# A three-term sum of w_down's weights made and stored during the up product, and a convolution tap moved from GpSimd to ScalarE

## What is computed

```python
def causal_depthwise_conv(u, w, b):
    C = u.shape[-1]
    y = lax.conv_general_dilated(u, w[:, None, :].astype(u.dtype), window_strides=(1,),
                                 padding=[(CONV_WIDTH - 1, 0)],
                                 dimension_numbers=('NWC', 'WIO', 'NWC'),
                                 feature_group_count=C)
    return y + b
...
        h = rms_norm(x, ffn_norm_g)
        u = causal_depthwise_conv(h @ w_up, conv_w, conv_b)
        gate, val = jnp.split(u, 2, axis=-1)
        x = x + (jax.nn.silu(gate) * val) @ w_down
```

## Time and profile before

| | us |
|---|---|
| median of 3 runs (1435.15 to 1435.22) | 1435.2 |
| the profiled execution | 1435.17 |
| its span, first to last instruction | 1433.3 |
| TensorE busy in the span | 1427.8 |
| VectorE busy | 1138.3 |
| ScalarE busy | 841.5 |
| GpSimd busy | 448.0 |

### The profile page before, as it was taken

How to read it: one execution, slowest core, us unless ns; L and a number is a source line. 1 busy time by engine, 2 the same in 40 slices (tenths; PEclk the granted TensorE clock), 3 DMA queues, 4 the chain that set the end, 5 groups by cost and what they waited for, 6 DMA issues and landing times.

```text
span 1433.3 us, 23700 instructions
## 1 busy us (share of the span) xinstructions
PE 1427.8 (100%) x7626; PEld 1222.9 (85%) x7626; DVE 1138.3 (79%) x1503; ACT 841.5 (59%) x1181; POOL 448.0 (31%) x493
## 2 busy tenths in 40 slices
PE   9999999999999999999999999999999999999999
PEld 7888888888888888888888888888888888888887
DVE  6778998886656566899967778777778778999998
ACT  7545667666767666666664455455554545465553
POOL 2310000333132213650025455655556555200000
PEclk9999999999999999999999999999999999999999
DMA  8565665655554545567555565566665565566664
GB/s 260 187 197 172 209 195 186 193 176 176 161 162 160 167 170 178 189 221 234 192 178 184 183 202 181 186 191 190 190 191 185 180 198 185 192 232 206 204 207 148
DMA packets 121063, 272.25 MB, mean 190 GB/s; under 512 B 10688, under 2 KB 10976, under 8 KB 121008
## 3 DMA queue, kind: packets, MB, share of 16 engines
q1 hardware_dynamic: 119936, 268.99, 58.1%
q0 software_dynamic: 896, 2.42, 0.6%
q10 hardware_dynamic: 176, 0.14, 0.0%
HBM read 269.42 MB, written 2.10 MB: 189 GB/s over the span
## 4 chain that ended last, share of the span: by engine, by line
PE 99%; DMA 0%; DVE 0%; DVEq 0%; issue 0%
PE bank L2098 98%; PE bank L2152 1%; DMA y<-in_x 0%; PE bank L2371 0%; PE bank L2412 0%; DVE y L1770 0%; PE bank L2235 0%; PE bank L2171 0%; PE bank L2213 0%; DVE y L1815 0%; DVEq L201 0%; PE bank L2220 0%; PE bank L2210 0%; PE bank L2202 0%; DVEq L529 0%
## 5 line engine op out<-in xcount | busy, mean ns | idle before, releaser
L1100 DVE TENSOR_TENSOR lo<-raw,hi 128x1024 fp32r<-128x1024 f32 (+1 forms) x342 | 444.3, 1304 | 167.0 <-ACT hi L639 166.3
L639 ACT ACTIVATE hi<-raw 128x1024 fp32r<-128x1024 f32 (+1 forms) x342 | 359.2, 1053 | 271.6 <-PE bank L2098 266.9
L2098 PE MATMUL bank<-h2T,hi 128*128 128x512 f32 x1408 | 483.3, 394 | 0.0
L2098 PE MATMUL bank<-h2T,lo 128*128 128x256 f32 x1408 | 376.8, 278 | 0.0
L2098 PEld LDWEIGHTS bank<-h2T,hi 128*128 128x128 f32 x1408 | 257.9, 188 | 53.5
L2098 PE MATMUL bank<-hT,hi 128*128 128x512 f32 (+1 forms) x784 | 272.9, 395 | 0.0
L2098 PEld LDWEIGHTS bank<-h2T,lo 128*128 128x128 f32 x1408 | 264.4, 188 | 7.8
L2098 PE MATMUL bank<-hT,lo 128*128 128x256 f32 (+1 forms) x784 | 212.6, 281 | 0.0
L2062 POOL TENSOR_TENSOR u<-u,rms_row 128x256 f32<-128x256 f32 x88 | 120.9, 1374 | 184.7 <-DVE u L1621 165.7
L2098 PE MATMUL bank<-hi,ffT 128*128 128x512 f32 x576 | 177.4, 389 | 0.0
L2098 PEld LDWEIGHTS bank<-hT,hi 128*128 128x128 f32 (+1 forms) x784 | 143.9, 187 | 29.4
(11 more groups left out here) (292 smaller groups left out, 2017.6 us busy)
## 6 DMA issues: line engine op xcount, KB each, us to landing
raw<-in_w_up SPq DMA_DIRECT2D x176, 512.0 KB, 3.5
raw<-in_w_in SPq DMA_DIRECT2D x160, 512.0 KB, 3.4
raw<-in_w_down SPq DMA_DIRECT2D x88, 512.0 KB, 4.4
raw<-in_w_branch SPq DMA_DIRECT2D x32, 512.0 KB, 3.6
raw<-in_w_out SPq DMA_DIRECT2D x24, 512.0 KB, 4.6
raw4h<-in_w_in SPq DMA_DIRECT2D x8, 512.0 KB, 3.4
raw5h<-in_w_in SPq DMA_DIRECT2D x8, 512.0 KB, 4.4
raw45m<-in_w_out SPq DMA_DIRECT2D x8, 512.0 KB, 4.9
```

The source lines that it names most:

```text
L639: act.activation(hi[s][:, 0:width], raw[s][:, 0:width], ACT.Copy)\
L1100: dve.tensor_tensor(lo[s][:, 0:width], raw[s][:, 0:width], hi[s][:, 0:width].bitcast(f32), ALU.subtract)\
L2098: return pe.matmul(o, l, r, start=start, stop=stop, skip_group_check=True)
```

## The change

Two things are changed. First, the weight sums of the pairs 8 to 15, for both halves m, are made during up: in each of the groups n = 1 to 8, SP loads the rows of one pair for each half into `pre0` and `pre1` (three DMAs, 1 MB each half), VectorE makes three sums in place (`pre_sums`), and SP stores them (1 MB each half) to a tensor `sums` in HBM. In down the 16 merged steps of these pairs (`stored`) load four chunks (256 KB and 3 x 512 KB) in place of two, and make no sums. Pairs 14 and 15 are merged as well, in both halves, by a sixth batch: 8 merged pairs in the first half, 12 in the second. Only the four merged pairs 0 to 3 of the second half still sum on VectorE. The order of steps is new: 5 plain pairs and then merged and plain in turn 8 times, one plain; the batches' due times are moved to match. Second, in up the third tap is no longer GpSimd's but an activation of ScalarE with the tap as scale (`last_tap`), which for a value tile adds the value bias in the same instruction (Identity with a bias); GpSimd keeps the scaling and the product with silu. The diff, cut to its core:

```diff
-               Batch(10, 2, (5, 0), (5, 1), (6, 0), (6, 1), (7, 0)),
-               Batch(12, 2, (9, 0), (10, 2), (12, 2), (13, 0), (14, 2)),
-               Batch(0, 2, (19, 0), (19, 1), (20, 0), (21, 0), (21, 1)),
-               Batch(2, 2, (25, 2), (27, 2), (29, 2), (30, 0), (31, 2))]
+               Batch(10, 2, (4, 1), (5, 2), (6, 0), (6, 1), (7, 2)),
+               Batch(12, 2, (8, 0), (8, 1), (9, 2), (10, 0), (10, 1)),
+               Batch(14, 2, (11, 2), (12, 0), (12, 1), (13, 2), (14, 0)),
+               Batch(0, 2, (15, 2), (16, 0), (16, 1), (17, 2), (18, 0)),
+               Batch(2, 2, (29, 2), (30, 0), (30, 1), (31, 2), (32, 0))]
     SUMMED = [b.pair + j for b in BATCHES for j in range(b.count)]
+    STORED_AT, STORED = 8, 8
...
-        first = [(0, k, None) for k in range(8)]
-        for i in range(6):
-            first += [(0, SUMMED[i], i), (0, 14 + i, None)]
-        first += [(0, k, None) for k in (20, 21)]
-        rest = [k for k in range(PAIRS) if k not in SUMMED]
-        second = [(1, rest[0], None)]
-        for i in range(10):
-            second += [(1, SUMMED[i], i), (1, rest[i + 1], None)]
-        second += [(1, rest[11], None)]
-        table, chunk = [], C_DOWN
-        for i, (m, pair, made) in enumerate(first + second):
-            table.append(Step(m, pair, made, chunk, 2 * i))
+        first = [(0, k, None) for k in range(5)]
+        for i, k in enumerate((5, 6, 7, 16, 17, 18, 19, 20)):
+            first += [(0, SUMMED[i], i), (0, k, None)]
+        first += [(0, 21, None)]
+        second = [(1, k, SUMMED.index(k) if k in SUMMED else None)
+                  for k in (6, 8, 0, 7, 9, 1, 16, 10, 17, 11, 18, 12, 2, 19, 13, 3, 20, 14, 21, 15,
+                            4, 5)]
+        table, chunk, raw = [], C_DOWN, 0
+        for m, pair, made in first + second:
+            stored = made is not None and STORED_AT <= pair < STORED_AT + STORED
+            table.append(Step(m, pair, made, chunk, raw, stored))
             chunk += 2 if made is None else 4
+            raw += 4 if stored else 2
...
+        pre = [at(f"pre{m}", [4 * GRP], (72 + 8 * m) * KB) for m in range(2)]
+        sums = nc.dram_tensor("sums", (2 * STORED * P, 4 * GRP), f32, kind="Internal").ap()
...
+            def pre_load(m, n):
+                wait_alone(sp, pre_stored[m], 16 * n - 15)
+                row, col = 2 * P * n + 2 * P * (STORED_AT - 1), m * BLOCK
+                sp.dma_start(pre[m][:, 0:2 * GRP], w_down[ds(row, P), col:col + BLOCK])\
+                    .then_inc(pre_landed[m], 16)
+                sp.dma_start(pre[m][:, 2 * GRP:3 * GRP],
+                             w_down[ds(row + P, P), col + GRP:col + BLOCK])\
+                    .then_inc(pre_landed[m], 16)
+                sp.dma_start(pre[m][:, 3 * GRP:4 * GRP], w_down[ds(row + P, P), col:col + GRP])\
+                    .then_inc(pre_landed[m], 16)
+            def pre_store(m, n):
+                wait_alone(sp, pre_summed, 6 * n - 3 + 3 * m)
+                sp.dma_start(sums[ds(P * n + (m * STORED - 1) * P, P), :], pre[m][:, :])\
+                    .then_inc(pre_stored[m], 16)
+            prime(sp, *pre_stored)
+            for b in range(2):
+                load_group(C_UP + b * CPG, w_up, 0, b * FF)
+            wait_alone(sp, rms_done, 2)
+            with sp.Fori(1, STORED + 1) as n:
+                for b in range(2):
+                    for j in range(CPG):
+                        if (b, j) in ((0, 0), (0, 4)):
+                            pre_load(j // 4, n)
+                        wait_alone(sp, lo_done, C_UP + b * CPG + j - AHEAD + 2 * CPG * n)
+                        rows = w_up[j * CK * P:(j + 1) * CK * P, ds(b * FF + GRP * n, GRP)]
+                        load(j % SLOTS, raw[j % SLOTS][:, :].rearrange("p (k c) -> p k c", k=CK),
+                             rows.rearrange("(k p) c -> p k c", p=P))
+                        if (b, j) in ((1, 3), (1, 7)):
+                            pre_store(j // 4, n)
+            for m in range(2):
+                wait_alone(sp, pre_stored[m], 16 * STORED + 1)
+            with sp.Fori(STORED + 1, NU) as n:
                 for b in range(2):
                     load_group(C_UP + b * CPG, w_up, 2 * CPG * n, b * FF + GRP * n)
...
+                width = GRP if step.stored and k == 0 else BLOCK
+                if k < 2:
                     kt = 2 * step.pair + k
-                    load(RAW_SLOT[q], raw_down[RAW_SLOT[q]][:, :],
-                         w_down[kt * P:(kt + 1) * P, step.m * BLOCK:(step.m + 1) * BLOCK])
+                    src = w_down[kt * P:(kt + 1) * P, step.m * BLOCK:step.m * BLOCK + width]
+                else:
+                    row = (step.m * STORED + step.pair - STORED_AT) * P
+                    src = sums[row:row + P, (k - 2) * BLOCK:(k - 1) * BLOCK]
+                load(slot, raw_down[slot][:, 0:width], src)
...
+            def last_tap(b, n, ct):
+                e = 4 * n + ct
+                scaled, done = ((gate_scaled, gate_w2), (val_scaled, val_w2))[b]
+                if b == 0 and (not isinstance(e, int) or e >= 2):
+                    act.wait_ge(silu_done, e - 1)
+                if b == 1 and ct >= 2:
+                    act.wait_ge(ffT_done, e - 1)
+                act.wait_ge(scaled, e + 1)
+                tap = params[:, ds(2 * KT + 2 * FT * 2 + b * FT + e, 1)]
+                if b == 0:
+                    act.activation(conv[b][ct % 2][:, :], u[b][ct][:, 2:S + 2], ACT.Copy,
+                                   scale=tap).then_inc(done, 1)
+                else:
+                    act.activation(conv[b][ct % 2][:, :], u[b][ct][:, 2:S + 2], ACT.Identity,
+                                   bias=params[:, ds(2 * KT + 3 * 2 * FT + FT + e, 1)],
+                                   scale=tap).then_inc(done, 1)
             def up_step(n, j):
 
                 if j < 4:
                     val_half(n - 1, j)
+                if j in (1, 3, 5, 7):
+                    last_tap(1, n - 1, j // 2)
...
+                if j in (1, 3, 5, 7):
+                    last_tap(0, n, j // 2)
...
+                if step.stored:
+                    down_hi(step.chunk + 2, weights_in(step.raw + 2))
+                    between(i, 2)
+                    down_hi(step.chunk + 3, weights_in(step.raw + 3))
+                    return
...
+                    if storing and j in (1, 2, 3, 5, 6, 7):
+                        pre_sums(j // 4, n, j % 4 - 1)
...
+            def pre_sums(m, n, k):
+                p = pre[m]
+                if k == 0:
+                    dve.wait_ge(pre_landed[m], 48 * n)
+                    dve.tensor_tensor(p[:, 0:2 * GRP], p[:, 0:2 * GRP], p[:, GRP:3 * GRP],
+                                      ALU.add).then_inc(pre_summed, 1)
+                if k == 1:
+                    dve.wait_ge(pre_summed, 6 * n - 5 + 3 * m)
+                    dve.tensor_tensor(p[:, 2 * GRP:3 * GRP], p[:, 0:GRP], p[:, 2 * GRP:3 * GRP],
+                                      ALU.add).then_inc(pre_summed, 1)
+                if k == 2:
+                    dve.wait_ge(pre_summed, 6 * n - 4 + 3 * m)
+                    dve.tensor_tensor(p[:, 3 * GRP:4 * GRP], p[:, 2 * GRP:3 * GRP],
+                                      p[:, 3 * GRP:4 * GRP], ALU.add).then_inc(pre_summed, 1)
             up_body(0, False)
-            with dve.Fori(1, NU) as n:
+            with dve.Fori(1, STORED + 1) as n:
+                up_body(n, True, True)
...
-            def column(first, e):
-                return params[:, ds(first + e, 1)].to_broadcast([P, S])
-            CONV_B = 2 * KT + 3 * 2 * FT
-            def begin(b, n, ct, ready, at_, done):
+            def scale_tile(b, n, ct, ready, at_):
 
                 e = 4 * n + ct
-                if not isinstance(e, int) or e >= 2:
-                    pool.wait_ge((silu_done, ffT_done)[b], e - 1)
                 pool.wait_ge(ready, at_ + e + 1)
                 pool.tensor_tensor(u[b][ct][:, 2:S + 2], u[b][ct][:, 2:S + 2], rms_row[:, :],
                                    ALU.mult).then_inc((gate_scaled, val_scaled)[b], 1)
-                pool.wait_ge((gate_scaled, val_scaled)[b], e + 1)
-                pool.tensor_tensor(conv[b][ct % 2][:, :], u[b][ct][:, 2:S + 2],
-                                   column(2 * KT + 2 * FT * 2 + b * FT, e), ALU.mult)\
-                    .then_inc(done, 1)
 
             def gate_tiles(n):
                 for ct in range(4):
-                    begin(0, n, ct, col_done, 64, gate_w2)
+                    scale_tile(0, n, ct, col_done, 64)
 
             def val_tiles(n):
                 for ct in range(4):
                     e = 4 * n + ct
                     c = conv[1][ct % 2][:, :]
-                    begin(1, n, ct, bcol_done, 16, val_w2)
+                    scale_tile(1, n, ct, bcol_done, 16)
                     pool.wait_ge(val_w0, e + 1)
-                    pool.tensor_tensor(c, c, column(CONV_B + FT, e), ALU.add)\
```

(50 more changed lines are left out.)

36 lines of the change are left out of this document (17 added, 19 removed).

## The result

The changed kernel takes 1445.18 us (median of 4 runs, 1442.79 to 1445.59), the kernel before 1435.21 in the same sessions: a ratio of 1.0063, 95% interval 1.0049 to 1.0078. It is slower by 10.0 us where 2.7 us less was forecast, and outside the stated range. The profiled execution took 1445.10 us. Its page: span, busy time of each engine, DMA share in 40 slices, and the chain that ended last.

What follows compares the result with a forecast made beforehand. The prediction took the kernel to be bound by TensorE's number of matmuls. 1435.17 us less 2.72 for 12 matmuls, all other costs 0, gives 1432.45, forecast as 1432.5 us (-0.19%), range 1432.2 to 1443.

Steps and rivals of the forecast that it cites:

- The gain: Down: four more merged pairs save 3 matmuls each, 12 matmuls at 0.227 us, 2.72 us.
- Cost 0 in the steady part: Down after its start: VectorE has 29 us less work, transfers run near 0.87 share, so TensorE loses nothing.
- E: Rival: the merge gives no fewer matmuls, or late loads in every stored down step cost over 0.35 us; chance 0.02.
- Down's start: Merged steps begin at step 5 instead of 8, so chunks are due earlier; bounds -0.1 to +2 us, taken 0.
- Rival C: Down's start stalls once by 0.5 to 2 us: 1433.0 to 1434.5 us, no measurable change; chance 0.12.
- Up, transfers: Storing groups: added loads and stores raise DMA share from 0.60 to 0.90, still covered by the buffers.
- rival A: Transfers set up's pace once added bytes cost over 1.33 times today's price; 1440 to 1450 us; chance 0.16.
- hi comes at most 3 us late: Up, at a group's end: queued transfers and VectorE's lag delay hi by at most 3 of 5.9 us available.
- Up, VectorE: Storing groups: sums add 5.2 us, VectorE 39.7 us busy of 44.4; the hi/lo ring covers the lag, cost 0.
- The conv chain: Up: with taps on ScalarE the value-tile chain takes 3.7 us, at most 4.9, under 5.5; worth 0, cover needed.
- Identity's table: Up, ScalarE: if Identity needs another table, two loads, 2.6 us in a 44.4 us group, stay hidden; cost 0.
- B: Rival: in up VectorE's lag outgrows the ring, 1.3 us in each of 8 groups, 1443 us; chance 0.09.

Runs made afterwards that it cites:

- experiment 1: Changed kernel, with down's second-half steps that make their own sums put ahead of their stored neighbours, behind a plain step: 1436.6 us, ratio 1.0007.
- experiment 2: Changed kernel with one VectorE addition to y moved one step later in down: 1442.64 us, ratio 1.0047.
- experiment 6: On top of experiment 1, six plain steps instead of five ahead of down's first merged step: 1434.47 us, ratio 0.9994.
- experiment 9: As experiment 7, with seven plain steps first and two places where stored steps stand side by side: 1434.43 us, ratio 0.9991.
- experiment 10: Changed kernel with the addition to y moved from the second to the third of the four self-summing steps: 1444.87 us, ratio 1.006.
- experiment 8: On top of experiment 1, no stores to HBM; stored steps load as many bytes of w_down instead: 1433.54 us, ratio 0.9986.
- experiment 5: On top of experiment 1, pre loads go out two chunks later in each group of up: 1434.37 us, ratio 0.9993.
- experiment 7: Changed kernel with the edits of experiments 1, 5 and 6 together: 1433.20 us, ratio 0.9984 to the kernel before.
- experiment 3: Kernel before with only third tap and value bias moved to ScalarE: 1434.93 us, ratio 0.9997.
- experiment 4: Changed kernel with third tap and value bias back on GpSimd: 1479.02 us, ratio 1.0301.

## Why the prediction was wrong, point by point

**The gain** was right: 12 matmuls less at 0.227 us.

**Down, "Cost 0 in the steady part": this is the step that failed.** It rested on an average (29 us less of VectorE's work over all of down) and not on what stands in its list between two given chunks. The average was mis-added too: 16 steps made sums before and 4 still do, so 12 x 2.6 us are saved and not 16 x 2.6, and 31.2 - 7.6 - 5 is 18.6. Measured are 18.3 (211.7 us busy before, 193.4 after). That slip alone cost nothing, for the waits come from four places in the list. Before, each step with sums had a plain one ahead of it, two chunks of 12 matmuls over 2.6 us of sums. The new order puts a stored step there, whose last chunks run 2.7 us for sums and a lo. It cost 4 x 1.65 us, 0.65 more for the addition and 1.6 for the clock, 8.9 of the 10.7 us. Experiment 1 shows the four places and experiment 2 the addition; that the clock fell is measured, why it did is open. No rival had it; E named a late load in every stored step, which is another place and another cause.

**Down's start**: bounds -0.1 to +2, value taken 0, measured 1.9. Rival C was right in place and price. The tightness was read rightly from the earlier trace rows, its reason half: not VectorE's list but raw was late. Ahead of both stalls hi had waited for a load (start, duration, instruction, and in brackets the idle time before it and what ended it):

```profile
1242.36 1.06 ACT L1104 ACTIVATE hi<-raw 128x1024 fp32r<-128x1024 f32 x1 [1.59 <-DMA raw<-sums]
...
1244.56 1.06 ACT L1104 ACTIVATE hi<-raw 128x1024 fp32r<-128x1024 f32 x1 [1.14 <-DMA raw<-in_w_down]
1244.73 0.30 PEld L2186 LDWEIGHTS bank<-hi,leftb 128*128 128x128 f32 x2 [0.95 <-DVE lo L1773]
...
1246.93 0.30 PEld L2186 LDWEIGHTS bank<-hi,ffT 128*128 128x128 f32 x2 [0.97 <-DVE lo L1773]
```

The ring of four under stored steps stood in the kernel's description; the 7.9 us that I gave each load hold for the ring of six. Starting the stored steps later moved these waits (experiments 6 and 9).

**Up, transfers**: cost taken 0, measured 2.2 in the profiled run and 4.5 in that of experiment 10. The share came out at 0.83 to 0.85 (0.9 said), a stored byte as a loaded one (experiment 8), so rival A's condition, 1.33 times the price, was not met, and transfers do not set the pace of up. All of A's signs came nevertheless (hi waiting for raw, late weight loads where one group ends and the next begins, fewer matmuls in a window of up), at 2.2 us and not at 7 or 18. What was off is the term "hi comes at most 3 us late": the hi at 977.45 started some 6.9 us later than three chunks (8.3 us) ahead of its matmuls, which were due at 978.9; 5.9 could be borne, and 1.0 is what TensorE waited. The other profiled runs fit. Of the kernels that have the taps on ScalarE and make the sums in up, the one with a longest wait for raw of 5.9 us lost 26 matmuls in the window of up (experiment 10), those with 5.6 and 5.0 lost 13 each (the change, experiment 2), those with 4.9, 4.9 and 4.5 lost 7, 4 and 4 (experiments 5, 6 and 1), and those with 3.8 or less lost 1 each (7, 8, 9), as experiment 3 did without any such wait. Why runs with the same code in up differ that much stays open. SP stood at no reuse of pre; it waited once, 5.6 us, for the last store ahead of group 9, and no weight load was late behind it.

**Up, VectorE**: right in its cost, 0. It was 36.3 to 37.9 us busy in a storing group (39.7 said), because the taps' move relieved it too: in experiment 3 it is 19 us less busy over the window of up, 1.9 in a group. The sums are dearer where GpSimd runs, and its product beside them:

```profile
L2171 POOL TENSOR_TENSOR conv<-conv,silu 128x256 f32<-128x256 f32 x40 | 64.5, 1613 | 119.0 <-DVE conv L1705 119.0
...
L1753 DVE TENSOR_TENSOR pre<-pre 128x1024 f32<-128x1024 f32 x16 | 21.7, 1354 | 0.0
L1757 DVE TENSOR_TENSOR pre<-pre 128x512 f32<-128x512 f32 x16 | 19.7, 1230 | 0.0
...
L1761 DVE TENSOR_TENSOR pre<-pre 128x512 f32<-128x512 f32 x16 | 10.9, 679 | 0.0
```

A 512-wide sum takes 1.23 us at L1757 and 0.68 at L1761, and GpSimd's product 1.61 where it took 0.79. That is the exclusion that the prediction took from the Trainium skill (SBUF — State Buffer, Who interferes with whom); the trace agrees (at 1082.27 us such a sum starts while a product of 1.65 us is under way), and the chain still fits, for its length of 3.7 us had room for it.

**The conv chain** was right, and more so than said: it was called the cover for the sums, and without it up loses 34 us (experiment 4).

**Identity's table**: no load of one beside the first silu's. That fits the page ScalarE: Activation LUTs of the Trainium skill (Table sets: the hidden batching unit), which has identity in every set.

**The range** ended at 1443, from rivals A and B. B did not happen and A only in its signs, at a fraction of its price; the 8.9 us of down's second half were priced nowhere. Slower had a chance of 0.27, for other reasons than the one that came.

## What to carry to other kernels

When work moves out of one step and the steps are reordered, read the in-order list of the busy engine between each pair of neighbouring steps, above all where the two kinds meet in an order that did not occur before; sums over a stage don't show it. A buffer that is refilled from HBM needs its release-to-use time at the narrowest ring, not at the usual one. And a change of two parts can need both: here the taps were worth nothing alone and 34 us beside the sums.

## What the runs showed of the hardware that was not expected

After a wait of 1.9 us and one of 0.6 within 3 us, TensorE was granted half its clock for about 3.4 us (seven matmuls 0.427 us apart): 1.6 us lost beside the 2.3 that the waits cost. The waits before these lay 16 us back. The same two waits 39 us later in another kernel (experiment 10), 36 us after the ones ahead of them, left the clock at 1.00, and so did all the waits of 1.3 + 0.6 us. In experiment 4 the same two waits, again 16 us behind the ones ahead of them, left it at 1.00 too. So neither the length of the waits nor their distance from earlier ones decides it by itself in these traces; what does stays open.

88 GB/s on top of 189 were moved at no higher price in DMA share (334 GB/s for a full share, 315 before). But the landing of a 512 KB load of up rose from 3.5 to 4.5 us, and there was more scatter: 10 runs of experiment 1 lie 4.7 us apart, 10 without the stores 1.3 us, and 19 of the kernel before 2.0 us.
